# Second layer's modulation summed on the vector engine inside the feed-forward stages, and an attention loop with three pairs in flight

## The reference

```python
for layer in range(2):
    mx = jnp.split(jax.nn.silu(c) @ ada_w[layer] + ada_b[layer], 9, axis=-1)
    mc = jnp.split((jax.nn.silu(c_ctx) @ ada_w[layer] + ada_b[layer])[None, :], 9, axis=-1)
    x = x + 0.5 * mx[2] * swiglu(modulate(rms_norm(x), mx[0], mx[1]), ffn1_w_gu[layer], ffn1_w_down[layer])
    # the same for ctx with mc; then q, k, v, pool and Fourier mixers on modulate(.., m[3], m[4])
    s = einsum(q, k) * scale; p = softmax(s); a = einsum(p, v)      # 8 heads, keys = x and ctx
    x = x + mx[5] * merge_mixers(a, u_pool, u_fft, ...)
    x = x + 0.5 * mx[8] * swiglu(modulate(rms_norm(x), mx[6], mx[7]), ffn2_w_gu[layer], ffn2_w_down[layer])
```

## Time and profile before

| | us |
|---|---|
| median of 3 runs (2352.47 to 2357.14) | 2354.18 |
| the profiled execution | 2349.65 |
| its span, first to last instruction | 2347.9 |

### The profile page before, as it was taken

One profiled execution on the slowest core, in us unless ns is written; L12 is line 12 of the kernel. 1 busy time (PEld: TensorE's weight loads), 2 busy tenths in 40 slices (PEclk: granted clock), 3 DMA queues, 4 the chain that ended last, 5 costly groups with the idle time before them and its releaser, 6 DMA issues.

```text
span 2347.9 us, 32138 instructions
## 1 busy us (share of the span) xinstructions
PE 2275.5 (97%) x13844; PEld 1829.4 (78%) x13844; DVE 1060.8 (45%) x1626; ACT 695.0 (30%) x950; POOL 198.3 (8%) x195
## 2 busy tenths in 40 slices
PE   7999999999999999999999999999999999989998
PEld 6778975555478888899459888888888888848998
DVE  5676534333364333352446333335433334446554
ACT  5444331111142212232444221213212222344333
POOL 2111210000010000120112000012000003012002
PEclk9999998999999999999999999999999999999999
DMA  9775887999953243232843323323323323444573
GB/s 291 259 266 181 287 305 292 420 421 420 398 151 97 80 120 90 75 96 77 319 142 90 91 86 110 100 75 97 108 80 109 95 73 115 152 169 133 165 203 110
DMA packets 371515, 407.81 MB, mean 174 GB/s; under 512 B 10841, under 2 KB 342094, under 8 KB 350126
## 3 DMA queue, kind: packets, MB, share of 16 engines
q1 hardware_dynamic: 356174, 326.07, 42.2%
q0 software_dynamic: 14896, 79.09, 9.2%
q10 hardware_dynamic: 304, 0.59, 0.1%
HBM read 404.66 MB, written 1.05 MB: 173 GB/s over the span
## 4 chain that ended last, share of the span: by engine, by line
PE 86%; DVE 7%; ACT 3%; DMA 2%; issue 1%; SPq 0%; POOL 0%; DVEq 0%; ACTq 0%
PE B L1739 23%; PE B L1741 22%; PE B L1740 22%; PE B L2118 6%; PE B L2138 3%; PE B L2088 2%; DMA HF<-in_ada_w 2%; PE B L1860 2%; PE B L2076 2%; ACT T L1667 1%; DVE LO L669 1%; DVE SM L1232 1%; DVE R L680 1%; DVE HF L1025 1%; DVE T L1245 1%; DMA XS<-in_ctx 1%
## 5 line engine op out<-in xcount | busy, mean ns | idle before, releaser
L1739 PE MATMUL B<-hH,HI 128*128 128x512 f32 (+1 forms) x1936 | 659.1, 340 | 14.0 <-DVE hL L1013 7.0
L1740 PE MATMUL B<-hL,HI 128*128 128x512 f32 (+1 forms) x1936 | 653.8, 338 | 0.0
L1741 PE MATMUL B<-hH,LO 128*128 128x512 f32 (+1 forms) x1936 | 653.7, 338 | 0.0
L669 DVE TENSOR_TENSOR LO<-RAW,HI 128x2048 fp32r<-128x2048 f32 (+3 forms) x218 | 443.8, 2038 | 121.2 <-ACT HI L1323 111.4
L1323 ACT ACTIVATE HI<-RAW 128x2048 fp32r<-128x2048 f32 (+3 forms) x218 | 368.6, 1692 | 356.6 <-PE B L1741 276.8
L1739 PEld LDWEIGHTS B<-hH,HI 128*128 128x128 f32 x1936 | 368.8, 190 | 60.0 <-DVE LO L669 11.9
L1741 PEld LDWEIGHTS B<-hH,LO 128*128 128x128 f32 x1936 | 368.9, 191 | 39.4
L1740 PEld LDWEIGHTS B<-hL,HI 128*128 128x128 f32 x1936 | 369.0, 191 | 38.4 <-issue 0.2
L1124 DVE TENSOR_TENSOR T<-B,T 128x512 f32<-128x512 f32 (+1 forms) x88 | 55.0, 625 | 492.4 <-PE B L1741 492.4
L1741 PE MATMUL B<-aH,LO 128*128 128x512 f32 (+1 forms) x770 | 269.3, 350 | 0.0
L1739 PE MATMUL B<-aH,HI 128*128 128x512 f32 (+1 forms) x770 | 269.0, 349 | 0.0
(11 more groups left out here) (353 smaller groups left out, 2631.8 us busy)
## 6 DMA issues: line engine op xcount, KB each, us to landing
RAW<-in_ffn_w_gu SPq DMA_DIRECT2D x176, 512.0 KB, 5.0
W<-in_w SPq DMA_DIRECT2D x78, 1024.0 KB, 11.5
HF<-in_ada_w POOLq DMA_DIRECT2D x48, 1024.0 KB, 7.8
W2T<-in_w SPq DMA_DIRECT2D x39, 1024.0 KB, 11.9
RAW<-in_w_in SPq DMA_DIRECT2D x60, 512.0 KB, 5.0
RAW<-in_ffn_w_down SPq DMA_DIRECT2D x56, 384.0 KB, 3.7
RAW<-in_ffn_w_down SPq DMA_DIRECT2D x56, 320.0 KB, 4.2
ADW<-in_ada_w POOLq DMA_DIRECT2D x16, 1024.0 KB, 10.8
```

The lines of the kernel that those rows point to most:

```text
L669: V.tensor_tensor(LO[s][:, :words], RAW[s][:, :words], HI[t.hi[s]][:, :words].bitcast(F32), ALU.subtract).then_inc(lo_done[s], 1)
L1739: mm(o, wh, xh, start=first, stop=False, **more)
L1740: mm(o, wh, xl, start=False, stop=False, **more)
L1741: return mm(o, wl, xh, start=False, stop=last, **more)
```

## The change

Two things change.

First, the layer-1 modulation leaves the mixers. The weights are taken in 72 units of 128 x 1024 (`mod_weights` on POOL, two places `MADW`). DVE multiplies each by the two per-partition values of `CS` and adds to two accumulators `MACC` (`mod_sum`). 24 units stand in each of the feed-forwards 0, 1 and 2, three vectors each: one unit in gate-and-up steps 1 to 8 of either half, and one in each of the first eight down steps of the first half. For each vector PE then sums over partitions with eight small matmuls (`mod_sums`), ACT copies 128 x 256 (`mod_copy`), PE turns it with two matmuls (`mod_turn`), DVE reads it (`mod_read`). `MADW` lies where the pooling table `POOL` lies, so the table is loaded again ahead of each `mixers` (`pool_tables`). `MACC` lies where `HF` lies.

Second, the attention loop has one round more and another order. PE issues transposes of pair u-3, scores of u, product of u-3. DVE does maximum u, scaling u-1, `XL` u-3. ACT does copies u-3, exp u-1, `XH` u-3. There are four score banks, and probability tiles for three pairs. The Fourier output (`FW`) is no longer computed ahead of the loop but in its first two rounds.

```diff
+            def mod_weights(n0, n1):
+                for n in range(n0, n1):
+                    m, k = n // KT, n % KT
+                    if n >= 2:
+                        pool.wait_ge(*mod_used(n - 2))
+                    pool.dma_start(MADW[n % 2][:], a["ada_w_2"][1][k * P:(k + 1) * P, MOD_W * m:MOD_W * (m + 1)])\
+                        .then_inc(ada_loaded[n % 2], 16)
...
             pool.wait_ge(E["acc_done"], 1)
-            pool.dma_start(POOL[:], a["pool_mix"]).then_inc(E["mix_consts_loaded"], 16)
+            mod_weights(0, 2)
...
+            units = MODS_PER_FFN * KT
+            mod_weights(2, units)
+            pool_tables(units)
             after_ffn(2)
-            pool.wait_ge(E["pf_ready"], 4)
-            ada_weights(ADA_UNITS, ADA_UNITS + 3 * KT)
+            pool.wait_ge(E["pool_done"], 2)
+            mod_weights(units, units + 2)
             even_squares_in_turn()
+            mod_weights(units + 2, 2 * units)
             after_ffn(2)
+            mod_weights(2 * units, 3 * units)
+            pool_tables(3 * units)
             after_ffn(2)
-            pool.wait_ge(E["v_ready"], 2)
-            ada_weights(ADA_UNITS + 3 * KT, 2 * ADA_UNITS)
...
+            def mod_sum(n):
+                k = n % KT
+                ve.wait_ge(ada_loaded[n % 2], 16 * mod_used(n)[1])
+                if n > 0:
+                    ve.wait_ge(*mod_used(n - 1))
+                for v in range(2):
+                    c = CS[:, k, v:v + 1]
+                    if k == 0:
+                        ins = V.tensor_scalar(MACC[v][:], MADW[n % 2][:], c, None, ALU.mult)
+                    else:
+                        ins = V.scalar_tensor_tensor(MACC[v][:], MADW[n % 2][:], c, MACC[v][:], ALU.mult, ALU.add)
+                ins.then_inc(ada_used[n % 2], 1)
...
                         if j > 0 or half > 0:
                             prep(FFN_CHUNKS[j + 1])
+                        if f is not None and half == 1 and j == 1:
+                            mod_read(MODS_PER_FFN * f + 1)
+                        if f is not None and 1 <= j <= KT:
+                            mod_sum(KT * (MODS_PER_FFN * f + 2 * half) + j - 1)
                         products()
...
+                    if f is not None:
+                        mod_read(MODS_PER_FFN * f + 2 * half)
...
                             prep(words)
+                        if f is not None and half == 0 and i < KT:
+                            mod_sum(KT * (MODS_PER_FFN * f + 1) + i)
                         products()
...
+            def mod_sums(m):
+                claim(6, "ada_copied", len(ADA_GROUPS) + m + 1)
+                pe.wait_ge(*mod_used(KT * (m + 1) - 1))
+                w = MOD_W // COL_TILES
+                for v in range(2):
+                    for j in range(COL_TILES):
+                        ins = mm(B[6][CT_W * j:CT_W * (j + 1), 0:w], PICK[:, v, :], MACC[v][:, w * j:w * (j + 1)],
+                                 start=(v == 0), stop=(v == 1))
+                ins.then_inc(E["mod_summed"], 1)
...
-                ada(FILL[3])
-                pe.wait_ge(E["ft_ready"], t.n["ft_ready"])
...
-                for u in range(len(pairs) + 2):
+                for u in range(len(pairs) + 3):
+                    if u >= 3:
+                        h, q0, k0, nk = pairs[u - 3]
+                        got("prob_ready")
+                        for c in range(2):
+                            claim(2 + c, "probT_ready", before + 2 * (u - 3) + c + 1)
...
+                            ins.then_inc(E["probT_done"], 1)
                     if u < len(pairs):
                         h, q0, k0, nk = pairs[u]
-                        banks = [SCORE_BANKS[(2 * u + c) % 3] for c in range(2)]
+                        banks = [SCORE_BANKS[(2 * u + c) % 4] for c in range(2)]
...
+                    if u < 2:
+                        pe.wait_ge(E["ft_ready"], t.n["ft_ready"])
+                        claim(2 + u, "mix_ready")
...
-                    if mix_unit(l, u):
-                        ada(1)
```

More of the change, by code:

```diff
@@ L241, in build @@
         DFT = at(61, "DFT", [P, 2, TB, S])
+        MACC = [at(45 + 4 * v, f"MACC{v}", [P, MOD_W]) for v in range(2)]
+        MADW = [at(53 + 4 * i, f"MADW{i}", [P, MOD_W]) for i in range(2)]
         TRIG = at(65, "TRIG", [P, 2, S])
@@ L250, in build @@
         HF32 = [nc.alloc_sbuf_tensor_at(f"HF32_{i}", [P, KT, 2 * S], F32, offset=h_at[i]) for i in range(2)]
-        ADW = [[h[:, :, S:] for h in HF32],
-               [h[:, k:k + 4, :].rearrange("p k (b n) -> p (k b) n", b=2) for h in HF32 for k in (0, 4)]]
-        ADW[0] += [at(64 + 8 * i, f"ADW{i}", [P, KT, S])[:] for i in range(2)]
+        ADW = [h[:, :, S:] for h in HF32]
+        ADW += [at(64 + 8 * i, f"ADW{i}", [P, KT, S])[:] for i in range(2)]
         HTH, HTL = hH[:, :, 0:S], hL[:, :, 0:S]
         HTS = [h[:, :, S:2 * S] for h in HF32]
-        ADT1 = at(73, "ADT1", [P, ADA_W])
-        ADT = [[T[2], T[5], T[5], T[4], T[2]], [ADT1] * len(ADA_GROUPS)]
+        MADT = at(73, "MADT", [P, MOD_W // COL_TILES])
+        PICK = at(74, "PICK", [P, 2, CT_W])
+        ADT = [T[2], T[5], T[5], T[4], T[2]]
         SC = [[T[0][:, 2 * P * i:2 * P * (i + 1)].rearrange("p (c n) -> p c n", c=2),
@@ L580, in ada_weights, with pool_tables @@
                         pool.wait_ge(ada_used[place], n // 4)
-                    rows = a["ada_w_2"][l][k * P:(k + 1) * P, c0:c0 + w]
-                    pool.dma_start(ADW[l][place][:, 0:w // S, :], rows.rearrange("p (b n) -> p b n", n=S))\
+                    rows = a["ada_w_2"][0][k * P:(k + 1) * P, c0:c0 + w]
+                    pool.dma_start(ADW[place][:, 0:w // S, :], rows.rearrange("p (b n) -> p b n", n=S))\
                         .then_inc(ada_loaded[place], 16)
+            def mod_weights(n0, n1):
[5 more added lines that the diff above has]
+                        .then_inc(ada_loaded[n % 2], 16)
+            def pool_tables(n):
+                for i in (1, 2):
+                    pool.wait_ge(*mod_used(n - i))
+                pool.dma_start(POOL[:], a["pool_mix"]).then_inc(E["mix_consts_loaded"], 16)
             def inputs_used():
@@ L1113, in into, with ffn @@
                     norm(l, shift, scale, 1, [], {})
-            def ffn(l, gate, n):
+            def ffn(l, gate, n, f=None):
                 sets = range(n // S)
+                if f == 0:
+                    ve.wait_ge(E["cs_ready"], 2)
+                    link(V.memset(PICK[:], 0.0))
+                    for v in range(2):
+                        V.memset(PICK[:, v, v:v + 1], 1.0)
                 for half in range(2):
@@ L1221, in mixers @@
                     turned(4)
-                for d in range(2):
-                    mix_split(B[2 + d][:, :n], 6 + d, 0, P, 0, n)
                 pairs = attention_pairs(l)
-                for u in range(len(pairs) + 2):
+                for u in range(len(pairs) + 3):
                     i = 2 * u % 4
@@ L1358, in _, with ada_copy, mod_copy @@
                     .then_inc(E["hf_ready"], 1)
[L1360 to L1362 removed]
+            def ada_copy(g):
+                last = (g + 1) * KT - 1
                 act.wait_ge(ada_used[last % 4], last // 4 + 1)
[L1364 removed]
+                A.activation(ADT[g][:, 0:ADA_GROUPS[g]], B[6][:, 0:ADA_GROUPS[g]], ACT.Copy).then_inc(E["ada_copied"], 1)
+            def mod_copy():
+                got("mod_summed")
+                A.activation(MADT[:], B[6][:, 0:MOD_W // COL_TILES], ACT.Copy).then_inc(E["ada_copied"], 1)
             def other_inputs():
@@ L1532, in _, with ffn @@
             norm(0, 0, 0)
-            def ffn(n, more):
+            def ffn(n, more, f=None):
                 for half in range(2):
@@ L1539, in ffn @@
                             prep(FFN_CHUNKS[j + 1])
+                        if f is not None and (j == FT_HALF - 1 or half == 1 and j == 0):
+                            mod_copy()
                         got("gate_done")
@@ L2407, in mixers @@
                         ins.then_inc(E["scores_done"], 1)
-                    if u >= 2:
-                        h, q0, k0, nk = pairs[u - 2]
+                    if u < 2:
+                        pe.wait_ge(E["ft_ready"], t.n["ft_ready"])
+                        claim(2 + u, "mix_ready")
+                        for p in range(2):
+                            ins = mm(B[2 + u][:, :n], FW[:, l, p, u * P:(u + 1) * P], T[2 + p][:, :n], start=(p == 0),
+                                     stop=(p == 1))
+                        ins.then_inc(E["yf_done"], 1)
+                    if u >= 3:
+                        h, q0, k0, nk = pairs[u - 3]
                         pe.wait_ge(E["probT_ready"], t.next("probT_ready", 2))
```

185 lines of the change are left out of this document (90 added, 95 removed).

## The result

| | before | after |
|---|---|---|
| median, us | 2353.3 (2350.0 to 2357.1) | 2316.7 (2313.5 to 2321.4) |
| profiled execution / its span | 2349.65 / 2347.9 | 2318.18 / 2315.6 |

The ratio is 0.9845, with a 95% interval of 0.9822 to 0.9869. In the two later comparisons the changed kernel had medians of 2316.05 and 2315.71 and ratios of 0.9848 and 0.9843. The forecast was 2317.

A forecast was written before the change was run, and what follows sets the result against it. PE was taken to bound the kernel, with the DVE-ACT round trip setting the attention loops. Gains of 52.1 us less 15.3 of new PE work gave 2312.9, plus 4.5 for the median 2317 us; range 2309 to 2323, chance 0.64.

The forecast's parts named there:

- What bounds the kernel: Whole kernel: PE 97% busy; in the attention loop units are hidden and the DVE-ACT round trip sets 4.37 us a round.
- Ahead of the loops: Before the loops: mixers(0) stretch 8.8 us instead of 17.4, gain 8.6; mixers(1) first scores after 6.3 us.
- The loop: Attention loop of mixers(0): 47.4 us against 68.6, gain 21.2; rounds of 3.2 us with 512 keys, 2.05 with 256.
- Mixers(1): Lead and loop of mixers(1): 37.8 us against 60.1, gain 22.3 us.
- What PE gets: Feed-forwards: sums and turns for nine vectors at 1.7 us each, 15.3 us, all on the path.
- What DVE and POOL get: Feed-forwards: 72 DVE units of 2.45 us, some 170 us, and POOL's 512 KB loads, all hidden.
- the slack at the third down chunk: Change from gate-and-up to down: DVE's `LO` is done at 798.4, PE needs it at 799.7, slack 1.3 us.
- Sum: Whole kernel: 2349.65 - 52.1 + 15.3 = 2312.9 us for an execution; median 4.5 above, 2317 us, 1.6% less.
- Rival (a): Loop rounds come to 3.6 and 2.5 us, or PE's small groups drain at 2.4: 2323 to 2333 us; chance 0.18.
- Rival (b): PE's clock falls to 1.2 GHz in the loops, 59 us if in all rounds, 2376 us; chance 0.04.
- Rival (c): Loads or DVE hold up PE in the feed-forwards, 20 to 40 us: 2337 to 2357 us; chance 0.06.
- Rival (d): Loop stays at 4.37 us a round, only the stretches ahead of the loops gain: 2349 us; chance 0.04.

The follow-up runs named there:

- the first try at a better fill: Changed kernel with the product going to bank 4 or 7 in turn and the Fourier output's `XH` and `XL` made one round later: 2318.9 us.

## Why the prediction was right

- **What bounds the kernel.** The reading of the earlier trace rows, that DVE and ACT take turns and the units are hidden, is shown by the old loop without units: 4.37 again.
- **Ahead of the loops.** In mixers(0) the end of the second pooling product and the first scores are at 1134.08 and 1142.80, 8.7 us; forecast 8.8. In mixers(1) they are at 2042.2 and 2048.2, 6.0; forecast 6.3.
- **The loop.** 48.35 us to the first matmul behind it, forecast 47.4; rounds of 3.10 (3.2) and 1.97 (2.05), mixed ones of 2.86 (2.7). The loop is 0.95 longer than I summed. The fill is not to blame: it took 7.6 (7.7), the table load included. The five rounds of 512 keys took 16.0 (16.0), the mixed ones 8.65 (8.1), the five of 256 keys 9.7 (10.25), which cancel. What was too small is the end: three rounds without scores and the last `XH` and `XL` took 6.5 us (5.25), because PE waits there for `XL` (0.89) and twice for copies (0.53). Gain of stretch and loop 28.9, forecast 29.8.
- **Mixers(1).** From feed-forward 2's end to the final transposes 328.1 before (2013.1 to 2341.2), 306.0 after: gain 22.1, forecast 22.3. From the second pooling product to the first matmul behind the loop it is 37.7, forecast 37.8.
- **What PE gets.** 15.3 us, forecast 15.3, shown by leaving it out.
- **What DVE and POOL get.** Nothing on the path: PE's waits in the feed-forwards are as short as before. DVE's busy time rose by 162 us, forecast 170. The forecast's own terms give 72 x 2.45 = 176; the units measured 155.8 + 12.7 = 168.5, as the first of a vector is a plain multiplication, 747 ns an instruction instead of 1278. Whether the slack at the third down chunk is 1.3 us stays open: doubled units began its `LO` 0.8 us later, and PE didn't wait.
- **Sum.** The changed part is 37.4 shorter; forecast 52.1 - 15.3 = 36.8. 1.6 us of it stood in no sum: PE's norm matmuls behind feed-forward 0 took 3.4 us instead of 5.0, at a granted clock that falls there in both kernels, but later in the changed one (1.00 in their first 2.4 us, where it was 0.83 before). In the twelve profiles that have units in feed-forward 0 these matmuls took 3.4 to 3.9 us, in the two without 5.0 and 5.2. So it may well belong to the change, but what the units do to the clock there stays open. Without it the gain would be 35.8, 1.0 under the forecast. That the median came out within 0.4 us of 2317 is luck: the forecast counted from a median of 2354.2, which is 2353.3 with one more execution, took 1.0 too much for the gain, and had nothing for these 1.6. The parts of the sum are what was read well.
- **Rival (a)** is out: the rounds are 3.11 and 1.97, not 3.6 and 2.5, and PE's groups came to 1.70 a vector, not 2.4. **Rival (b)** did not happen, clock 1.00 in the loop; but its mechanism is real: in the old loop without units, and in the first try at a better fill, PE's groups took 1.7 and 1.8 times as long after waits. In the changed kernel PE hardly waits. Short waits alone didn't bring it either: with the transposes behind the scores PE waited 1.1 us in every 512-key round, and the granted clock stayed at 1.00. **Rival (c)**: POOL issued 72 loads at 534 ns each beside DVE's two-input work, they landed in 3.9 us, and even at one load ahead PE didn't notice. The contention of the earlier trace rows is one of POOL's arithmetic and was not seen in its issues. **Rival (d)** is out.

## What to carry to other kernels

Read a loop that several engines share as rings of waits, and count what each ring goes through; a ring is opened by order and by depth together, and here order alone gave nothing and depth alone two fifths at most. Work hidden in a loop that waits is free only as long as the loop waits: move it out in the same change that makes the loop tight, and into an engine whose idle time lies inside a stage that another engine bounds. Where executions differ by more than an edit is worth, compare a fixed stretch of the traces instead of medians.

## What I had not expected of the hardware

- Filler work kept the clock. With its units the old loop's window from 1190 to 1220 had a granted clock of 1.00; without them 1210 to 1220 had 0.69, and the stage behind it was 2.6 us longer. The loop with two pairs in flight left the same mark: 0.69 from 1205 to 1215. The loop with three pairs and the transposes behind the scores had no filler either and kept 1.00 to its end.
- DVE can be filled without a gap from one chunk to the next, 7.23 us of work in a chunk that takes PE 7.6 to 7.7, and PE's time for feed-forward 0 stays at 395.9 us against 396.0.
